# Moving the high and low parts of the weights by 64 bytes in a split-precision transformer kernel

## The chip, the core and the metric

The kernel runs on one core of a Trainium2 chip. The metric is device time in microseconds (us) of one execution, and a kernel's time is the median of its runs. One execution was also recorded by the hardware profiler; all rows below come from it. Engines are named as in the profile: PE (matmul; PEld is its weight load), DVE (vector), ACT (scalar), POOL, SP (here it issues the weight DMAs).

## What is computed

Two transformer blocks in float32, one after the other, on 256 tokens of width 2048; the second adds 16 meta tokens in front.

```python
def first_block(x, c, ...):
    mod = silu(c) @ ada_w + ada_b                     # six vectors: shifts, scales, gates
    h = rms_norm(x) * (1 + sc1) + sh1
    y = hybrid_mixer(h, w_in, ..., w_out)             # attention, gated causal convolution
    x = x + g1 * rms_norm(y)
    h = rms_norm(x) * (1 + sc2) + sh2
    y = (silu(h @ w_gate) * (h @ w_up)) @ w_down      # 2048 -> 5632 -> 2048
    return x + g2 * rms_norm(y)

def second_block(x, meta_tokens, ...):
    r = concatenate([meta, x])                        # 272 rows
    mix = mixer_block(rmsnorm(r), w_in, ..., w_attn_o, pool_w, w_pool_o, w_out)
    r = r + rmsnorm(mix)
    a = causal_dwconv(rmsnorm(r) @ w_up)              # gate and value, 5632 each
    ff = (gelu(gate) * val) @ w_down
    return (r + rmsnorm(ff))[:, 16:]
```

Nearly all the work is the products with the weight matrices.

## The kernel before

Activations lie transposed, features on the 128 partitions and tokens along the free dimension, so a weight tile of 128x128 is the stationary operand of a matmul and 256, 258 or 272 tokens are streamed past it. For float32 accuracy each product is made of three matmuls in the type fp32r: weights and activations are both split into a high part and a low part, and the kernel adds high times high, high weights times low activations, and low weights times high activations.

**The ring.** Weights come in halves of 128x1024 float32 (512 KB): four k-tiles of 256 columns. A half passes three buffers of the same shape, `raw`, `w_hi` and `w_lo`, each a ring of `RING` = 4 slots of 4096 bytes per partition:
- SP loads it into a slot of `raw` (`half`, L340), as soon as the low part that was made from the slot's last content is there.
- ACT copies it, rounded, to `w_hi` (`convert`, L518), once PE is through with the slot.
- DVE subtracts: `w_lo` = `raw` - `w_hi` (L996).
- PE runs 24 matmuls on it: four k-tiles, two column tiles of 128 each, three matmuls each. `half` (from L1591) and `half_one` (from L1730) do so; they differ in where the results go. The three lines are, in order, `w_hi` with high activations, `w_hi` with low activations, `w_lo` with high activations.

There are 836 halves. Before each matmul PE loads its weight tile (128 columns, 512 bytes per partition); the load of the next tile runs while the activations of the matmul before are streamed.

**The order of the work.** Each engine runs its own program, written out by hand, and engines wait for one another by semaphores. Nothing is chosen by a scheduler. The stages and their halves are:

| stage | halves | streamed tiles | columns |
|---|---|---|---|
| first block: gated input, then queries, keys, values | 32 + 48 | `h_hi`, `h_lo` | 256 |
| first block: output projection, attention part | 16 | `a1_hi`, `a1_lo` | 256 |
| first block: output projection, convolution part | 16 | `c_hi`, `c_lo` | 256 |
| first feed-forward: gate and up | 176 | `h_hi`, `h_lo` | 258 |
| first feed-forward: down | 88 | `hid_hi`, `hid_lo` (last chunk `_b`) | 256 |
| second block: queries, keys, values, pool input, forget gate | 66 | `h_hi`, `h_lo` | 272 |
| second block: gates | 64 | `h_hi`, `h_lo` | 258 |
| second block: pool weights and pool projection | 2 + 16 | `pl_hi`, `pl_lo` | 258 |
| second block: attention projection | 16 | `a_hi`, `a_lo` | 258 |
| second block: output projection | 32 | `m_hi`, `m_lo` | 258 |
| second feed-forward: gate and up | 176 | `h_hi`, `h_lo` | 258 |
| second feed-forward: down | 88 | `hid_hi`, `hid_lo` (last chunk `_b`) | 256 |

A feed-forward goes in 11 chunks: gate (8 halves) and up (8 halves) of a chunk, and down (8 halves) of the chunk before.

**Where the buffers lie.** One arena in SBUF holds everything large. It is cut into regions one behind the other: `raw`, `hi`, `lo`, `xt`, `hhi`, `hlo`, `r1`, `r2`, `r3` (L137 to L143), and `place` (L145) puts a tensor at an offset in a region. All sizes before are multiples of 256 bytes, so a tensor's start modulo 256, counted from the arena's start, is that of its offset. Small tensors come behind the arena.
- `raw`, `w_hi` and `w_lo` start at 0 in their regions, and a weight tile starts at a multiple of 512 in them.
- `h_hi`, `h_lo`, `c_hi`, `c_lo`, `a_hi`, `a_lo` have tiles of 272 tokens, 1088 bytes apart: 64 more modulo 256 with each. The 256 real tokens begin 64 bytes into a tile, the 258 live ones 56 bytes.
- `a1_hi`, `a1_lo` have tiles 1024 bytes apart: all at 0.
- `m_hi`, `m_lo`, `pl_hi` and `pl_lo` have tiles 1032 bytes apart: 8 more modulo 256 with each; `pl_lo` begins at 64.
- The tiles of `hid_hi` and `hid_lo` are placed one by one, by the first tuple below in the first feed-forward and by the second in the second; the bases 12288, 16640, 0 and 4352 are multiples of 256.

```python
HID_STEPS = ((192, 1216, 2240, 3264), (160, 1200, 2256, 3296))
```

Of the kernel before, what the change touches and what calls it, by code (L numbers as in the profile page):

```python
# [7 lines left out]
KT = D // 128  # L8
SEQ, META = 256, 16
ALL = SEQ + META  # L10
# [13 lines left out]
RING = 4  # L24
# [104 lines left out]
def build(nc, tokens, params, conv_taps, f_bias, ada_w, w_in, w_out, w_gate, w_up, w_down, w_in_2, w_f_2,  # L129
          w_attn_o_2, pool_w_2, w_pool_o_2, w_out_2, w_ffn_up_2, w_ffn_down_2, out):  # L130
    f32, f32r = mybir.dt.float32, mybir.dt.float32r
    ACT, ALU, AX = mybir.ActivationFunctionType, mybir.AluOpType, mybir.AxisListType
    ctx = ExitStack()
    with ctx:

        base = (nc.sbuf_base + 31) // 32 * 32
        sizes = dict(raw=RING * 4096, hi=RING * 4096, lo=RING * 4096, xt=KT * ALL * 4,  # L137
                     hhi=KT * ALL * 4, hlo=KT * ALL * 4, r1=KT * ALL * 4, r2=38400, r3=40960)
        at, region = 0, {}
        for name, size in sizes.items():  # L140
# [4 lines left out]
        def place(name, reg, off, shape, dt=f32):  # L145
            n = 4
            for s in shape[1:]:
                n *= s
            spans = {"hhi": ("hhi", "hlo")}.get(reg, (reg,))
            assert off + n <= sum(sizes[r] for r in spans), name  # L150
            return nc.alloc_sbuf_tensor_at(name, shape, dt, offset=base + region[reg] + off, align_bytes=4)
# [5 lines left out]
            return ctx.enter_context(nc.semaphore(name))  # L157

        raw = place("raw", "raw", 0, [128, RING, 4, 256])
        w_hi = place("w_hi", "hi", 0, [128, RING, 4, 256], f32r)  # L160
        w_lo = place("w_lo", "lo", 0, [128, RING, 4, 256], f32r)
        xt = place("xt", "xt", 0, [128, KT, ALL])
        h_hi = place("h_hi", "hhi", 0, [128, KT, ALL], f32r)
# [1856 lines left out]
```

## Time and profile before

| | us |
|---|---|
| median of 3 runs | 2722.62 |
| lowest and highest run | 2720.02, 2722.8 |
| profiled execution, its own time | 2717.04 |
| its span, first to last instruction | 2715.2 |
| PE busy in the span | 2609.8 (96%) |
| PE weight loads | 2482.3 (91%) |
| DVE busy | 1707.2 (63%) |
| ACT busy | 1220.3 (45%) |

Busy PE time counts overlapping matmuls once. A matmul's row gives 0.28 us, but the next one starts after some 0.12 us, so how fast PE goes is read from the starts and from how many matmuls stand in a stretch. A window's count has two or three more than started in it, since it takes in those that had begun before.

### The profile page before, as it was taken

How to read it: one execution, taken by the hardware profiler on the slowest of the kernel's cores; microseconds unless marked ns; L12 is line 12 of the kernel's file. 1: busy time of each engine (PE TensorE's matmuls, PEld its weight loads, DVE VectorE, ACT ScalarE, POOL GpSimd, SP SyncE). 2: the span in 40 equal slices, each digit the busy share in tenths (PEclk: the TensorE clock that was granted, in tenths of full speed). 3: DMA queues.
4: the chain of work that ended last, by engine and by line, in shares of the span. 5: the costliest groups of instructions: out<-in, count | busy, mean ns of one | idle time of the engine just before them, and what ended most of it. 6: DMA issues, size and time to landing. Idle time of an engine off the chain costs nothing.

```text
span 2715.2 us, 53794 instructions
## 1 busy us (share of the span) xinstructions
PE 2609.8 (96%) x21278; PEld 2482.3 (91%) x21278; DVE 1707.2 (63%) x2393; ACT 1220.3 (45%) x1649; POOL 49.3 (2%) x98
## 2 busy tenths in 40 slices
PE   5899999899999999998999999999899999999997
PEld 1588887899999999998998899999899999999997
DVE  1388864586666666657655655555676666666667
ACT  1343454544444444445544454444554444444444
POOL 0000000000000000000000000000000000000000
PEclk9799999999999999999999999999999999999999
DMA  9988867576666666565444455555465555555554
GB/s 403 375 309 297 275 204 271 164 244 202 201 203 202 202 202 201 181 185 176 140 145 142 132 155 185 181 182 184 126 193 182 184 184 183 182 183 185 185 173 132
DMA packets 137087, 545.51 MB, mean 201 GB/s; under 512 B 15120, under 2 KB 17424, under 8 KB 124560
## 3 DMA queue, kind: packets, MB, share of 16 engines
q1 hardware_dynamic: 127312, 474.08, 53.5%
q0 software_dynamic: 9216, 67.11, 6.9%
q10 hardware_dynamic: 448, 2.75, 0.3%
q8 instruction: 81, 1.33, 0.2%
q14 instruction: 30, 0.25, 0.0%
HBM read 541.78 MB, written 2.10 MB: 200 GB/s over the span
## 4 chain that ended last, share of the span: by engine, by line
PE 90%; DVE 4%; ACT 3%; DMA 3%; issue 1%; ACTq 0%; DVEq 0%; SPq 0%
PE bank L1608 20%; PE bank L1609 19%; PE bank L1610 19%; PE bank L1745 9%; PE bank L1746 8%; PE bank L1747 8%; PE bank L1644 2%; DMA ada_pre<-in_ada_w 2%; DVE w_lo L996 1%; PE bank L1685 1%; ACT w_hi L518 1%; DVE y L1061 1%; ACT h_hi L594 1%; DMA bf<-in_f_bias 0%; PE bank L1703 0%
## 5 line engine op out<-in xcount | busy, mean ns | idle before, releaser
L996 DVE TENSOR_TENSOR w_lo<-raw,w_hi 128x1024 fp32r<-128x1024 f32 x836 | 1012.5, 1223 | 725.5 <-ACT w_hi L518 724.7
L518 ACT ACTIVATE w_hi<-raw 128x1024 fp32r<-128x1024 f32 x836 | 872.8, 1057 | 914.5 <-PE bank L1610 517.2
L1608 PE MATMUL bank<-h_hi,w_hi 128*128 128x258 f32 (+2 forms) x4112 | 1170.8, 285 | 29.3 <-DVE h_lo L1067 20.4
L1609 PE MATMUL bank<-h_lo,w_hi 128*128 128x258 f32 (+2 forms) x4112 | 1170.2, 285 | 0.0
L1610 PE MATMUL bank<-h_hi,w_lo 128*128 128x258 f32 (+2 forms) x4112 | 1166.1, 284 | 0.0
L1608 PEld LDWEIGHTS bank<-h_hi,w_hi 128*128 128x128 f32 x4112 | 777.7, 189 | 47.4 <-DVE h_lo L1067 22.0
L1610 PEld LDWEIGHTS bank<-h_hi,w_lo 128*128 128x128 f32 x4112 | 779.5, 190 | 0.0
L1609 PEld LDWEIGHTS bank<-h_lo,w_hi 128*128 128x128 f32 x4112 | 779.1, 189 | 0.1
L1746 PE MATMUL bank<-hid_lo,w_hi 128*128 128x256 f32 x1280 | 356.7, 279 | 0.0
L1745 PE MATMUL bank<-hid_hi,w_hi 128*128 128x256 f32 x1280 | 356.5, 279 | 0.0
L1747 PE MATMUL bank<-hid_hi,w_lo 128*128 128x256 f32 x1280 | 356.5, 279 | 0.0
L1746 PEld LDWEIGHTS bank<-hid_lo,w_hi 128*128 128x128 f32 x1280 | 240.9, 188 | 0.0
L1745 PEld LDWEIGHTS bank<-hid_hi,w_hi 128*128 128x128 f32 x1280 | 240.8, 188 | 0.0
L1747 PEld LDWEIGHTS bank<-hid_hi,w_lo 128*128 128x128 f32 x1280 | 240.8, 188 | 0.0
L1306 DVE TENSOR_TENSOR y<-y,bank 128x512 f32<-128x512 f32 x176 | 120.6, 685 | 56.0 <-PE bank L1747 55.5
L1745 PE MATMUL bank<-h_hi,w_hi 128*128 128x256 f32 x384 | 111.0, 289 | 0.0
L1746 PE MATMUL bank<-h_lo,w_hi 128*128 128x256 f32 x384 | 107.1, 279 | 0.0
L1747 PE MATMUL bank<-h_hi,w_lo 128*128 128x256 f32 x384 | 106.9, 278 | 0.0
L1745 PEld LDWEIGHTS bank<-h_hi,w_hi 128*128 128x128 f32 x384 | 72.1, 188 | 16.8 <-issue 15.9
L1644 PE MATMUL bank<-ada_pre,cact 128*32 128x512 f32 x256 | 44.8, 783 | 33.0 <-DMA ada_pre<-in_ada_w 33.0
L758 ACT ACTIVATE hid_hi<-hid 128x256 fp32r<-128x256 f32 x80 | 31.4, 418 | 97.8 <-DVE hid L1329 62.5
L1746 PEld LDWEIGHTS bank<-h_lo,w_hi 128*128 128x128 f32 x384 | 72.2, 188 | 0.1
(225 smaller groups left out, 2637.0 us busy)
## 6 DMA issues: line engine op xcount, KB each, us to landing
raw<-in_w_in SPq DMA_DIRECT2D x208, 512.0 KB, 4.1
raw<-in_w_ffn_up SPq DMA_DIRECT2D x176, 512.0 KB, 4.2
ada_raw<-in_ada_w POOLq DMA_DIRECT2D x64, 1024.0 KB, 6.7
raw<-in_w_gate SPq DMA_DIRECT2D x88, 512.0 KB, 4.0
raw<-in_w_up SPq DMA_DIRECT2D x88, 512.0 KB, 4.2
raw<-in_w_down SPq DMA_DIRECT2D x88, 512.0 KB, 4.2
raw<-in_w_ffn_down SPq DMA_DIRECT2D x88, 512.0 KB, 4.4
ada_pre<-in_ada_w SPq DMA_DIRECT2D x32, 1024.0 KB, 8.6
```

The source lines that it names most:

```text
L518: act.activation(w_hi[:, slot], raw[:, slot], ACT.Copy).then_inc(hi_ready, 1)
L594: act.activation(h_hi[:, kt, cols], xt[:, kt, cols], ACT.Copy, scale=gain[:, kt:kt + 1])\
L758: act.activation(hi[t + o][:, :], hid[:, t + o], ACT.Copy).then_inc(hid_hi_ready, 1)
L996: dve.tensor_tensor(w_lo[:, slot], raw[:, slot], fp(w_hi[:, slot]), ALU.subtract).then_inc(lo_ready, 1)
L1306: dve.tensor_tensor(y[:, 2 * j:2 * j + 2, SB], y[:, 2 * j:2 * j + 2, SB], both(b), ALU.add)\
L1608: pe.matmul(dst, wh, x_hi(kt), start=first and k == 0, stop=False)
L1609: pe.matmul(dst, wh, x_lo(kt), start=False, stop=False)
L1610: mm = pe.matmul(dst, wl, x_hi(kt), start=False, stop=last and k == len(kts) - 1)
L1644: mm = pe.matmul(bank[32 * g:32 * g + 32, b, :], cact[:, kt:kt + 1].to_broadcast([128, 32]), rows[:, slot, 512 * g:512 * g + 512], start=k ...
L1745: pe.matmul(dst, wh, x_hi(kt), start=first and k == 0 and o == 0, stop=False, skip_group_check=True)
L1746: pe.matmul(dst, wh, x_lo(kt), start=False, stop=False, skip_group_check=True)
L1747: mm = pe.matmul(dst, wl, x_hi(kt), start=False, stop=end, skip_group_check=True)
```

## The change

`w_hi` begins 64 bytes into its region. The region `hi` grows by 64 bytes, so `lo` and with it `w_lo` begins 64 bytes further too, and `lo` grows by 192, so that `xt` and all behind it move by 256 bytes. `raw` stays where it is.

```diff
-        sizes = dict(raw=RING * 4096, hi=RING * 4096, lo=RING * 4096, xt=KT * ALL * 4,
+        sizes = dict(raw=RING * 4096, hi=RING * 4096 + 64, lo=RING * 4096 + 192, xt=KT * ALL * 4,
                      hhi=KT * ALL * 4, hlo=KT * ALL * 4, r1=KT * ALL * 4, r2=38400, r3=40960)
...
-        w_hi = place("w_hi", "hi", 0, [128, RING, 4, 256], f32r)
+        w_hi = place("w_hi", "hi", 64, [128, RING, 4, 256], f32r)
         w_lo = place("w_lo", "lo", 0, [128, RING, 4, 256], f32r)
```

The instructions of every engine, their order and their waits are the same in both programs; only addresses differ.

## Rows read from the trace of the kernel before

**Rows 1.** The page: busy time, granted clock by fortieths, and the chain that ended last.

```profile
PE 2609.8 (96%) x21278; PEld 2482.3 (91%) x21278; DVE 1707.2 (63%) x2393; ACT 1220.3 (45%) x1649; POOL 49.3 (2%) x98
...
PEclk9799999999999999999999999999999999999999
...
PE 90%; DVE 4%; ACT 3%; DMA 3%; issue 1%; ACTq 0%; DVEq 0%; SPq 0%
PE bank L1608 20%; PE bank L1609 19%; PE bank L1610 19%; PE bank L1745 9%; PE bank L1746 8%; PE bank L1747 8%; PE bank L1644 2%; DMA ada_pre<-in_ada_w 2%; DVE w_lo L996 1%; PE bank L1685 1%; ACT w_hi L518 1%; DVE y L1061 1%; ACT h_hi L594 1%; DMA bf<-in_f_bias 0%; PE bank L1703 0%
```

**Rows 2.** PE by stretches: length, busy time (matmuls), granted clock, DMA share, GB/s.

```profile
core 0: us, PE busy (x), PEclk, DMA share, GB/s
0.00:100.00 100.00, 58.55 (x304) 0.84 0.96 392
...
396.00:507.00 111.00, 107.50 (x858) 0.98 0.77 262
...
525.00:1280.00 755.00, 750.17 (x6364) 0.99 0.62 199
...
1930.00:2696.00 766.00, 758.62 (x6362) 1.00 0.55 176
2696.00:2715.20 19.20, 3.13 (x18) 0.70 0.32 109
```

**Rows 3.** PE in a down chunk of each feed-forward, a gate/up stretch, the last projection.

```profile
602.95:624.72 21.77, 21.77 (x195) 1.00 0.61 196
2011.12:2033.86 22.74, 22.74 (x194) 1.00 0.63 200
624.72:670.60 45.88, 45.88 (x387) 1.00 0.62 205
1832.19:1923.95 91.76, 91.76 (x770) 1.00 0.59 184
```

**Rows 4.** Timeline of PE, a half of the output projection on `a1`: start, length.

```profile
464.61 0.28 PE L1745 MATMUL bank<-a_hi,w_hi 128*128 128x256 f32 x1
464.73 0.28 PE L1746 MATMUL bank<-a_lo,w_hi 128*128 128x256 f32 x1
...
467.37 0.28 PE L1747 MATMUL bank<-a_hi,w_lo 128*128 128x256 f32 x1
```

**Rows 5.** Timeline of PE, a half of the first input projection on `h`.

```profile
229.08 0.28 PE L1745 MATMUL bank<-h_hi,w_hi 128*128 128x256 f32 x1
...
229.67 0.28 PE L1747 MATMUL bank<-h_hi,w_lo 128*128 128x256 f32 x1
229.78 0.28 PE L1745 MATMUL bank<-h_hi,w_hi 128*128 128x256 f32 x1
...
230.37 0.27 PE L1747 MATMUL bank<-h_hi,w_lo 128*128 128x256 f32 x1
...
230.72 0.28 PE L1747 MATMUL bank<-h_hi,w_lo 128*128 128x256 f32 x1
...
231.06 0.28 PE L1747 MATMUL bank<-h_hi,w_lo 128*128 128x256 f32 x1
...
231.76 0.28 PE L1747 MATMUL bank<-h_hi,w_lo 128*128 128x256 f32 x1
```

**Rows 6.** Weight loads (PEld), by streamed tile: duration in ns, min/median/max.

```profile
L1745 PEld LDWEIGHTS bank<-a_hi,w_hi x128: 186/192/192, 396.7 to 505.7; 128*128 128x128 f32 x128
L1745 PEld LDWEIGHTS bank<-hid_hi,w_hi x1280: 187/188/193, 602.8 to 2673.8; 128*128 128x128 f32 x183
L1745 PEld LDWEIGHTS bank<-h_hi,w_hi x384: 186/188/192, 211.8 to 395.2; 128*128 128x128 f32 x192
```

**Rows 7.** The conversions, by tile (ns, min/median/max) and by line (busy, mean; idle before).

```profile
L518 ACT ACTIVATE w_hi<-raw x836: 1039/1060/1072, 97.7 to 2686.5; 128x1024 fp32r<-128x1024 f32 x168
L996 DVE TENSOR_TENSOR w_lo<-raw,w_hi x836: 1204/1224/1311, 98.8 to 2687.6; 128x1024 fp32r<-128x1024 f32 x168
...
L996 DVE TENSOR_TENSOR w_lo<-raw,w_hi 128x1024 fp32r<-128x1024 f32 x836 | 1012.5, 1223 | 725.5 <-ACT w_hi L518 724.7
L518 ACT ACTIVATE w_hi<-raw 128x1024 fp32r<-128x1024 f32 x836 | 872.8, 1057 | 914.5 <-PE bank L1610 517.2
```

**Rows 8.** What instructions on `w_hi` sat idle for: us, times.

```profile
  PE bank L1747: 382.8, 220
...
  DVE w_lo L996: 11.5, 6
```

## The prediction

> **What bounds the kernel now.** I read the busy shares first. PE is busy 96% of the span, DVE 63%, ACT 45%, and PE's granted clock is at its upper level, 2.4 GHz, in all but the first and the last stretches [rows 1, 2]. The chain that ended last is PE for 90% of the span, and nearly all of that is the six matmul lines of `half` and `half_one` (L1608 to L1610 and L1745 to L1747) [rows 1]. So time is the number of matmuls with ring weights times their pitch, which I take as the distance from one matmul's start to the next one's start. There are 836 halves of 24 matmuls, 20,064 in all: 1 ns more or less on each of them is 20 us, 0.74% of the span. The durations in the rows (276 to 283 ns) are no help here, since matmuls overlap; the starts are.
>
> I then looked at whether the pitch is one number, and it is not. "Distance" below is the start of the streamed tile less the start of the weights, modulo 256. The code gives it without an absolute address, since all region sizes are multiples of 256 bytes.
> - The first feed-forward's down product streams `hid_hi`/`hid_lo` tiles that all lie at distance 192. Its 192 matmuls of a chunk take 21.77 us: 113.4 ns each [rows 3].
> - The second feed-forward's down product runs the same lines with the same 256 columns on tiles at distances 160, 176, 208 and 224: 22.74 us for 192, 118.4 ns [rows 3].
> - The first output projection streams `a1_hi`/`a1_lo`, all at distance 0. From 464.61 to 467.37 there are 23 steps in 2.76 us: 120.0 ns [rows 4].
> - The tiles of `h` are 1088 bytes apart, so they go through four distances, six matmuls on each. In the half that starts at 229.08 they are 64, 128, 192 and 0. Within distance 64 five steps take 0.59 us, within distance 128 five steps take 0.59 us (229.78 to 230.37): 118 ns each. Within distance 192 the last three steps (230.72 to 231.06) take 0.34 us: 113 ns, once more the figure of the down product at 192 [rows 5].
>
> Between the best and the worst of these there are 6.6 ns a matmul at the same clock and the same number of columns, and they go with where the streamed tile starts. L1745 to L1747 write the same PSUM pattern in both the 113.4 and the 120.0 case. DVE and ACT come and go during a chunk, and the pitch does not. What is left is the weights that PE reads at the same time. One row speaks for that directly: the median load of a weight tile takes 192 ns while the `a1` tiles at distance 0 stream, and 188 ns with the `hid` and `h` tiles [rows 6]. The weight tile has the same place in all of them. Only the stream beside it moved, and the load became slower. So I take pitch to be a function of the **distance** between the two, and the change lowers every distance by 64.
>
> **The change part by part**, against the profiled execution (2717.04 us, span 2715.2). Its own time lies 5.6 us under the median of the runs, 2722.62, and I add the sum to the median at the end.
>
> 1. Down product of the first feed-forward: 11 chunks of 8 halves, 2112 matmuls. Distance 192 becomes 128. Pitch now 113.4 [rows 3]; the nearest row for the new distance is the stretch of `h` at 128, 118 ns [rows 5]. It is on the path in full, since one matmul follows the other without idle time in the chunk. 4.6 ns x 2112 = **+9.7 us**.
> 2. Output projection on `a1`: 16 halves, 384 matmuls. Distance 0 becomes 192, so 120.0 becomes 113.4: 6.6 ns x 384 = **-2.5 us**. PE is busy 107.5 of 111 us in that stage [rows 2], so it counts.
> 3. Down product of the second feed-forward: 2112 matmuls, distances 160, 176, 208, 224 become 96, 112, 144, 160. No row has these. The bounds are the best and the worst stretch, 113.4 and 120.0, from 118.4: -10.6 to +3.4 us. I take 118.0, the row at distance 128, which is the middle of the four: **-0.8 us**.
> 4. Everything that streams `h` or `c` tiles (gate and up of both feed-forwards, both input projections, the gates of the second block), and `a` in the second block: the four distances go round in steps of 64, so a shift by 64 gives the same four, in the same cyclic order, beginning one tile later. Their pitch now is 45.88 us for 384, 119.5 ns at 258 columns [rows 3]. **0**, if only the distance counts. This is the largest assumption, since these are over 14,000 of the matmuls: 0.5 ns on them would be 7 us.
> 5. `m` in the last projection (768 matmuls, 91.76 us, 119.5 ns [rows 3]) and `pl` (384, with 48 more for the pool weights): the tiles are 8 bytes apart modulo 256, `m` at distances 0 to 120, which become 192 to 56. Half of these distances are in the row already. The other half (192 to 248) is bounded by 113.4 and 120 again: about 600 matmuls, -3.7 to +0.3 us. I take **0**.
> 6. ACT and DVE: the conversions read `raw` and write `w_hi`, read both and write `w_lo`, each from starts that are now 64 bytes apart. All 836 of each lie within 1039 to 1072 and 1204 to 1311 ns [rows 7], and nothing in the trace shows another distance for them. Within 5% either way they stay hidden: DVE waits 724.7 us for ACT, ACT 900 us for PE to free the slot, and PE waits for `w_lo` 11.5 us in all, in six waits [rows 7, 8]. 60 ns on six exposed waits is 0.4 us. **0**.
> 7. The weight DMAs land in `raw`, which does not move; no instruction is added, removed or reordered; all other buffers move by 256 bytes, and the pitch at 120 does not differ between starts a multiple of 256 apart. **0**.
>
> Sum: 9.7 - 2.5 - 0.8 = **+6.4 us**. Own range, with terms 3 and 5 at their ends: 9.7 - 2.5 - 10.6 - 3.7 = -7 to 9.7 - 2.5 + 3.4 + 0.3 = +11.
>
> The Trainium skill ("SBUF — State Buffer", "SBUF: two separate sides", and the bandwidth table behind it) says that PE has ports of its own that wait for no one, with a second independent read port for weight loads. By that rule moving the weights would do nothing, and the sum would be 0. The 192 against 188 ns of the load [rows 6] speaks against it here, though no run of before has the weights elsewhere. It is the first rival.
>
> **The rivals.**
> - **Only the streamed tile's own place counts** (or something else that this change leaves). Then weights may lie anywhere, every pitch stays, and the time is 2722.6. For it: every row has the weights at one place, so the trace cannot separate distance from place. Against it: the same stream length, lines and PSUM pattern give 113 and 120 ns, and the load of an unmoved weight tile changes with the stream. Chance 0.16.
> - **The second down product falls on a good distance.** The same mechanism, with term 3 (and the new half of term 5) near 113.4: -10.6 and -3.7 beside +9.7 and -2.5 gives -7 us, 2715.5. A step of 6.6 ns between distances 64 bytes apart is seen, so a place between 96 and 160 can be that good. Against: the two measured neighbours on this side, 64 and 128, are both at 118. The point from which it decides is 117.9 ns less 3 ns: under about 115.4 ns there the sum is negative. Chance 0.15.
> - **More than the distance counts: the start of the weights itself.** Slower, by much. The weights then begin 64 bytes off what they were in a memory whose pieces may be larger than 64 bytes, and each 512-byte tile touches one piece more. A price for touching more comes from the width: 258 columns on `h` take 119.5 ns [rows 3] and 256 columns 116.5 (23 steps from 229.08 to 231.76 [rows 5]); two columns in 256 are 0.9 ns of that, so 2 ns are left over for the longer and oddly placed run. Half of that, for a load that is the shorter of the two reads, on 20,064 matmuls is +20 us: 2743. It decides from 0.3 ns per matmul on. For it: term 4 stands on symmetry and on no row. Against: streams that begin at 64 and at 192 are no slower than those at 0 and 128. Chance 0.14.
> - The change does what it says: sizes and offsets shift exactly the two tensors by 64 and all behind them by 256. A rival is not needed there.
>
> **How the numbers follow.** The forecast has 0.55: 2722.6 + 6.4 = 2729. A change under 0.2% (5.4 us) cannot be told from none. Of the forecast's 0.55, 0.32 lies over +5.4 us, 0.2 within, 0.03 under -5.4. The first rival is within (0.16), the second is faster (0.13) or within (0.02), the third slower (0.14). Together: faster 0.16, same 0.38, slower 0.46. The range runs from the second rival's 2715 to a little over the third's centre, 2744, which leaves out about 0.1 above, and 0.05 to 0.1 below.
>
> **What the profile of the changed kernel would show.** Step 1: a chunk of the first down product takes 22.6 us in place of 21.77. Step 2: the `a1` steps are 113 ns, and their weight loads 188 ns. Step 3: the second down product's chunk, anywhere from 21.8 to 23.0 us. Step 4: 384 matmuls of gate and up still take 45.9 us. This is the row to look at first, since it holds most of the matmuls: if it moved, distance alone was not the whole story. Step 6: medians of 1060 and 1224 ns. If the chunk of step 1 stays at 21.77 and `a1` at 120, the weights' place does not matter. The prediction is wrong outside 2715 to 2744.

## The result, and the profile after

| | before | changed |
|---|---|---|
| median (12 runs each) | 2718.45 us | 2730.76 us |
| lowest and highest | 2713.99, 2726.89 | 2724.79, 2732.22 |
| ratio | | 1.0038 (95%: 1.0028 to 1.0047) |
| span of the profiled execution | 2715.2 us | 2723.6 us |

The changed kernel is slower by 0.38%, some 10 us. (The medians lie 12.3 us apart, the means of the runs 10.1.) The predicted time was 2729, from +6.4 us on a median of 2722.6; the median of before over these 12 runs is 2718.45.

The busy shares and the chain are those of before. The first two lines are the chain, the last two the conversions (busy, mean ns, idle before).

```profile
PE 90%; DVE 4%; ACT 3%; DMA 3%; issue 1%; ACTq 0%; DVEq 0%; SPq 0%
PE bank L1608 20%; PE bank L1609 19%; PE bank L1610 19%; PE bank L1745 9%; PE bank L1747 9%; PE bank L1746 9%; PE bank L1644 2%; DMA ada_pre<-in_ada_w 2%; DVE w_lo L996 1%; PE bank L1685 1%; ACT w_hi L518 1%; DVE y L1061 1%; DMA bf<-in_f_bias 1%; ACT h_hi L594 1%; PE bank L1703 0%
...
L996 DVE TENSOR_TENSOR w_lo<-raw,w_hi 128x1024 fp32r<-128x1024 f32 x836 | 1012.5, 1223 | 724.2 <-ACT w_hi L518 723.4
L518 ACT ACTIVATE w_hi<-raw 128x1024 fp32r<-128x1024 f32 x836 | 873.4, 1057 | 922.4 <-PE bank L1610 512.7
```

ACT and DVE do the same work in the same time as in [rows 7]. What moved is the distance between matmul starts. Three stretches of PE after: a down chunk of the first and of the second feed-forward, and 384 matmuls of gate and up. They answer to the first three lines of [rows 3].

```profile
600.34:623.12 22.78, 22.78 (x194) 1.00 0.61 187
2020.01:2042.69 22.68, 22.68 (x195) 1.00 0.63 201
623.12:669.01 45.89, 45.89 (x387) 1.00 0.64 205
```

The first down chunk went from 21.77 to 22.78 us (118.6 ns). Over all 11 chunks the steps add up to +11.4 us, since the ninth lost more than the others (see below). The second went from 22.74 to 22.68: -0.7 us. Gate and up kept their 45.9 us. The `a1` half (timeline: start, length), which answers to [rows 4]:

```profile
464.34 0.28 PE L1745 MATMUL bank<-a_hi,w_hi 128*128 128x256 f32 x1
...
466.94 0.28 PE L1747 MATMUL bank<-a_hi,w_lo 128*128 128x256 f32 x1
```

23 steps in 2.60 us are 113 ns, where [rows 4] has 2.76 us and 120. That would be -2.6 us for 16 halves. Halves that begin after a stop take a few steps to reach the 113 ns, and over all steps of the stage the sum is -2.2 us. The weight loads of `a1` fell from a median of 192 ns in [rows 6] to 188, the figure of the others:

```profile
L1745 PEld LDWEIGHTS bank<-a_hi,w_hi x128: 186/188/190, 397.3 to 504.3; 128*128 128x128 f32 x128
```

I added up the steps within each half over the whole trace, with halves that contain a stop put in at the mean of the others. All stages together give +8.5 us. With the steps between halves taken in as well (all steps under 200 ns) it is +9.7; the stops between are 2.3 us shorter and the first of these matmuls begins 0.9 us later, which makes the 8.4 us by which the span grew.

### The profile page after: what moved, and what is told of

The parts are those of the page before. It is cut to its first block, busy times and chain, and to the rows that moved or that the text cites. A ratio compares the mean times of both kernels' runs of the same rounds, so it can differ in the third digit from the quotient of the medians.

```text
span 2723.6 us, 53794 instructions
## 1 busy us (share of the span) xinstructions
PE 2616.1 (96%) x21278; PEld 2489.6 (91%) x21278; DVE 1707.2 (63%) x2393; ACT 1220.9 (45%) x1649; POOL 49.3 (2%) x98
## 4 chain that ended last, share of the span: by engine, by line
PE 90%; DVE 4%; ACT 3%; DMA 3%; issue 1%; ACTq 0%; DVEq 0%; SPq 0%
PE bank L1608 20%; PE bank L1609 19%; PE bank L1610 19%; PE bank L1745 9%; PE bank L1747 9%; PE bank L1746 9%; PE bank L1644 2%; DMA ada_pre<-in_ada_w 2%; DVE w_lo L996 1%; PE bank L1685 1%; ACT w_hi L518 1%; DVE y L1061 1%; DMA bf<-in_f_bias 1%; ACT h_hi L594 1%; PE bank L1703 0%
## 5 line engine op out<-in xcount | busy, mean ns | idle before, releaser
L1746 PE MATMUL bank<-hid_lo,w_hi 128*128 128x256 f32 x1280 | 360.0, 281 | 0.0
L1747 PE MATMUL bank<-hid_hi,w_lo 128*128 128x256 f32 x1280 | 359.8, 281 | 0.0
L1745 PE MATMUL bank<-hid_hi,w_hi 128*128 128x256 f32 x1280 | 359.5, 281 | 0.0
L1745 PEld LDWEIGHTS bank<-hid_hi,w_hi 128*128 128x128 f32 x1280 | 241.2, 188 | 0.0
L1746 PEld LDWEIGHTS bank<-hid_lo,w_hi 128*128 128x128 f32 x1280 | 240.8, 188 | 0.0
L1747 PEld LDWEIGHTS bank<-hid_hi,w_lo 128*128 128x128 f32 x1280 | 240.8, 188 | 0.0
L1745 PE MATMUL bank<-h_hi,w_hi 128*128 128x256 f32 x384 | 110.8, 289 | 0.0
L1747 PE MATMUL bank<-h_hi,w_lo 128*128 128x256 f32 x384 | 107.4, 280 | 0.0
L1746 PE MATMUL bank<-h_lo,w_hi 128*128 128x256 f32 x384 | 107.3, 280 | 0.0
L1745 PEld LDWEIGHTS bank<-h_hi,w_hi 128*128 128x128 f32 x384 | 72.2, 188 | 16.8 <-issue 15.9
L1746 PEld LDWEIGHTS bank<-h_lo,w_hi 128*128 128x128 f32 x384 | 72.4, 188 | 0.1
```

The costliest lines, as they stand in the source:

```text
L1745: pe.matmul(dst, wh, x_hi(kt), start=first and k == 0 and o == 0, stop=False, skip_group_check=True)
L1746: pe.matmul(dst, wh, x_lo(kt), start=False, stop=False, skip_group_check=True)
L1747: mm = pe.matmul(dst, wl, x_hi(kt), start=False, stop=end, skip_group_check=True)
```

## The experiments

In all of them "distance" is the start of the streamed tile less that of the weights, modulo 256, as in the prediction. A ratio is that to the kernel before, with its 95% interval. Where there was one run, it stands beside the median of before taken with it, and I rely on the trace alone. The window rows have the columns of [rows 3].

### Does the distance count, or the place? (arena_64)

```diff
-        base = (nc.sbuf_base + 31) // 32 * 32
+        base = (nc.sbuf_base + 31) // 32 * 32 + 64
...
-        ctx.enter_context(nc.sbuf_tensor("arena", [128, at + 32], mybir.dt.uint8))
+        ctx.enter_context(nc.sbuf_tensor("arena", [128, at + 96], mybir.dt.uint8))
```

> Every buffer of the kernel before, raw and the weights and the streamed tiles and the small ones, begins 64 bytes further, so all distances are those of before while all places modulo 256 are new. Distance theory: the kernel before again, first down chunk 21.77 us, second 22.74, a1 steps 120.0 ns, time within 0.1% (2718 us). Rival, the weights' own place modulo 256 counts (or modulo 128): the first down chunk goes to the 22.8 us of the changed kernel and the time to about 2729 us.

2717.41 us, ratio 0.9993 (0.9982 to 1.0005). The two down chunks:

```profile
601.37:623.14 21.77, 21.77 (x194) 1.00 0.65 196
2009.55:2032.29 22.74, 22.74 (x194) 1.00 0.66 201
```

They are those of before to the hundredth, and the steps of all stages together differ by less than 0.1 us. Here the weights have the places of the changed kernel modulo 256, and nothing is slower. So this place of the weights costs nothing by itself; what the change did, it did through the places of weights and streams against one another.

### Which of two weights does a stream meet? (hi_only_64)

The diff is that from the kernel before.

```diff
-        sizes = dict(raw=RING * 4096, hi=RING * 4096, lo=RING * 4096, xt=KT * ALL * 4,
+        sizes = dict(raw=RING * 4096, hi=RING * 4096 + 256, lo=RING * 4096, xt=KT * ALL * 4,
...
-        w_hi = place("w_hi", "hi", 0, [128, RING, 4, 256], f32r)
+        w_hi = place("w_hi", "hi", 64, [128, RING, 4, 256], f32r)
```

> w_hi alone begins 64 bytes further; w_lo keeps its place modulo 256, and so does all else. In the down product of the first feed-forward (streams at distance 192 from unmoved weights: 113.4 ns per matmul before, 118.8 with both parts moved) the two kinds of weights now lie at distances 128 (w_hi) and 192 (w_lo). Theory A, a stream collides with the weight load that runs beside it, which is that of the next matmul: the steps that follow L1745 and L1747 (next load from w_hi) are near 119, the step that follows L1746 (next load from w_lo) near 113; a chunk takes about 22.4 us. Theory B, a stream is slowed by where its own weights lie: the steps after L1745 and L1746 (own weights w_hi) are near 119, the one after L1747 near 113; the chunk takes the same 22.4 us, but the slow steps are others. Theory C, only the difference between w_hi and w_lo or the average over a triple counts: all three steps alike. Whole kernel: about +6 us against before for A and B.

2729.53 us in one run, before 2719.04. The first down chunk takes 22.78 us and gate and up 45.98:

```profile
601.27:624.05 22.78, 22.78 (x194) 1.00 0.64 189
624.05:670.03 45.98, 45.98 (x386) 1.00 0.64 204
```

Both theories A and B missed. Neither has its slow and fast steps: the means over the first chunk by line are 119.0 (after L1745), 119.2 (L1746) and 117.8 ns (L1747), with no step under 115. That the three are nearly alike is what theory C said, and no more than that. It is no average of the two distances either, since 128 for `w_hi` and 192 for `w_lo` give 22.78 us, as much as 128 for both. The stages on `h` lost 1.6 ns at 256 columns and 0.4 at 258, the four distances now being mixed in pairs. The one run is 10.5 us over before, where about 6 was expected. A step's length may then depend on the steps before it, and the next experiments take that up.

### Restoring the distance does not restore the pitch (w64_hid64, w64_hid_both)

Both start from the changed kernel. The diff is that of w64_hid_both; w64_hid64 has the first tuple alone.

```diff
-HID_STEPS = ((192, 1216, 2240, 3264), (160, 1200, 2256, 3296))
+HID_STEPS = ((256, 1280, 2304, 3328), (256, 1280, 2304, 3328))
```

> The changed kernel, with the hid tiles of the first feed-forward 64 bytes further too, so that their distance to the weights is 192 again. Distance theory: the first down chunk is back at 21.77 us (11.4 us less in all), a1 stays at 113.3 ns (2.5 us less than before), the second down product as in the changed kernel (0.4 us less than before): about 2.9 us under before, 2716 us. If the weights' own place costs something in the down product, the chunk stays near 22.8 us and the time near 2729 us.

> As w64_hid64, and the hid tiles of the second feed-forward lie at distance 192 as well. Distance theory: its down chunk goes from 22.70 to 21.77 us, 0.93 us in each of 11 chunks, 10 us less: about 13 us under before, 2705 us (-0.5%). If the second feed-forward's down product has a bound of its own (DVE does more there), its chunk stays over 22 us.

w64_hid64: 2730.67 us, ratio 1.0044 (1.0028 to 1.0061). w64_hid_both: 2725.82 us, 1.0025 (1.0016 to 1.0035). The first and second down chunk, of w64_hid64 and then of w64_hid_both:

```profile
600.56:623.18 22.62, 22.62 (x195) 1.00 0.64 191
2022.66:2045.34 22.68, 22.68 (x195) 1.00 0.64 198
```

```profile
599.96:622.58 22.62, 22.62 (x195) 1.00 0.62 190
2022.10:2044.72 22.62, 22.62 (x195) 1.00 0.67 204
```

This is the miss that taught most. At distance 192 the down product takes 22.62 us, 117.8 ns, in three places where I expected 21.77, while the `a1` stretch of the same kernels, also at distance 192, has its 113.3 ns. So a distance has more than one steady pitch. How a chunk begins shows it. Timeline of PE, the kernel before, then w64_hid64; the first row is the first matmul on a hid tile, after a stretch of 258 columns on `h`:

```profile
602.95 0.28 PE L1745 MATMUL bank<-hid_hi,w_hi 128*128 128x256 f32 x1
...
603.41 0.28 PE L1746 MATMUL bank<-hid_lo,w_hi 128*128 128x256 f32 x1
...
603.87 0.28 PE L1747 MATMUL bank<-hid_hi,w_lo 128*128 128x256 f32 x1
```

```profile
600.56 0.28 PE L1745 MATMUL bank<-hid_hi,w_hi 128*128 128x256 f32 x1
...
601.03 0.28 PE L1746 MATMUL bank<-hid_lo,w_hi 128*128 128x256 f32 x1
...
601.50 0.28 PE L1747 MATMUL bank<-hid_hi,w_lo 128*128 128x256 f32 x1
```

Steps 5 to 8 take 0.46 us in the one and 0.47 in the other. In nanoseconds the trace has 118, 116, 114, 113, 114, 113 in the first and 122, 115, 117, 118, 118, 117 in the second, and each keeps its pitch for the 192 matmuls. The code and the distance modulo 256 are the same. One thing that differs is the stretch before: it ends at distance 248 in the kernel before and at 184 with the weights moved. That is theory E: how the streams stand to each other when a stretch begins decides which of two cycles it falls into.

One chunk speaks for an effect of the entry with nothing moved. The ninth down chunk of the first feed-forward is entered not from `h` but from eight small matmuls of 4 columns. The first rows show them, in the timeline of the changed kernel, and the last seven halves (168 matmuls) of the chunk behind them. The next three have these halves in w64_hid64, in the kernel before and in hid_160_224, a run described below.

```profile
1150.86 0.95 PE L1658 MATMUL bank<-ident,rows_sb 128*128 128x4 f32 x8
...
1154.63:1174.79 20.16, 20.16 (x171) 1.00 0.59 183
```

```profile
1153.41:1173.20 19.79, 19.79 (x171) 1.00 0.62 185
```

```profile
1148.96:1168.00 19.04, 19.04 (x170) 1.00 0.63 192
```

```profile
1153.82:1173.76 19.94, 19.94 (x171) 1.00 0.58 184
```

In the changed kernel the same tiles at distance 128 run at 120.0 ns in this chunk and at 118.6 in the eight before it; at distance 160 it is 118.7 and 117.3. So one set of places has more than one pitch at these distances too. But the same chunk speaks against the two ends named above, 248 and 184, as the whole reason: here the small matmuls stand between, and w64_hid64 still runs at 117.8 and the kernel before at 113.3.

A rival is left. The changed kernel and all that start from it also move everything behind the weights by 256 bytes. Modulo 512 the high hid tiles are at distance 192 and the low ones at 448 in the kernel before, and the other way round in w64_hid64. No run tells this from the entry.

w64_hid64's ratio stands for 12 us (8 to 17), and its steps for 6.5. Some of the rest is seen in its trace: the granted clock was 0.98 in the projections of the second block, where it was 1.00 before, and the stage took 3.1 us longer. The first row is w64_hid64's, the second the one of before for the same halves.

```profile
1328.32:1540.54 212.22, 210.16 (x1556) 0.98 0.47 144
```

```profile
1321.44:1530.59 209.15, 207.07 (x1556) 1.00 0.47 146
```

Why the clock fell there I did not find out. w64_hid_both has the same dips.

### Entry against place (w64_first128, w64_parity)

Another rival to theory E is theory P: in the hid tiles, high and low part lie an odd multiple of 256 bytes apart, and in the `a1`, `h` and `c` tiles an even one. The first kernel gives each half another entry, the second takes that difference away. Both start from the changed kernel.

```diff
-HID_STEPS = ((192, 1216, 2240, 3264), (160, 1200, 2256, 3296))
+HID_STEPS = ((192, 1280, 2304, 3328), (160, 1200, 2256, 3296))
```

```diff
-HID_STEPS = ((192, 1216, 2240, 3264), (160, 1200, 2256, 3296))
+HID_STEPS = ((256, 1280, 2304, 3328), (160, 1200, 2256, 3296))
...
-        hid_parts = [[hid_tiles(f"hid_{name}_{part}", reg, first, HID_STEPS[part])
+        hid_parts = [[hid_tiles(f"hid_{name}_{part}", reg, first - 256 * (name == "hi" and part == 0), HID_STEPS[part])
```

> As w64_hid64 (first down product at distance 192, 117.8 ns where 113.4 was expected), but the first of the four hid tiles lies at distance 128, the other three at 192. Theory E, distance 192 has two steady pitches, 113.3 and 117.8, and which of them a stretch falls into depends on what it comes from: entered from distance 128 it goes 122, 116, 114, 113 as in the input projection before, so the twelve last matmuls of each half run at 113 and a half's mean is near 115.3 ns (chunk 22.1 us). Theory P, in this place 192 is simply worth 117.8 (the high and low tiles lie 256 bytes apart modulo 512, or some other place counts): the mean stays at 117.8 or above (chunk 22.6 us or more).

> As w64_hid64, but the high hid tiles of the first feed-forward's main chunks begin 256 bytes earlier, so that high and low tiles have the same place modulo 512, as the a1, h and c tiles have. Theory P (modulo 512 counts between high and low tile): first down chunk at 21.77 us, 113.4 ns. Theory E (entry decides): nothing of that counts, 117.8 ns again, 22.62 us.

One run each: 2719.27 and 2721.68 us, before 2719.74. The first down chunk of w64_first128, and a half of it; then the chunk of w64_parity:

```profile
601.96:624.09 22.13, 22.13 (x194) 1.00 0.60 192
```

```profile
604.73 0.28 PE L1745 MATMUL bank<-hid_hi,w_hi 128*128 128x256 f32 x1
...
605.44 0.28 PE L1745 MATMUL bank<-hid_hi,w_hi 128*128 128x256 f32 x1
...
606.13 0.28 PE L1745 MATMUL bank<-hid_hi,w_hi 128*128 128x256 f32 x1
...
607.49 0.28 PE L1745 MATMUL bank<-hid_hi,w_hi 128*128 128x256 f32 x1
```

```profile
600.24:622.86 22.62, 22.62 (x195) 1.00 0.64 192
```

P falls, and what E says of the entry is borne out: three of the four tiles have not moved against w64_hid64. Entered from distance 128, they are in the fast cycle, 12 steps from 606.13 to 607.49 in 1.36 us, 113.3 ns; entered as there, they take 117.8. Here a tile at the poor distance 128 (six steps in 0.71 us) makes the down product shorter by 5.4 us than four tiles at the good one (22.13 against 22.62 us, eleven times). Taking the odd 256 bytes between high and low away did nothing, 22.62 us again. It brought the high tiles alone back to distance 192 modulo 512, so that rival stays open for the low ones; the places do not settle the pitch, but they may have a say in which cycle an entry leads to.

### One distance for all k-tiles (rows_128, rows_120)

From the kernel before; rows_120 has OFF = 120 and the hid tiles 8 bytes earlier. The diff shows the main lines: the region sizes, the subtraction on DVE and the matmuls of PE are fitted to the new layout too.

```diff
+ROW = RING * 256 + 16
+OFF = 128
...
-HID_STEPS = ((192, 1216, 2240, 3264), (160, 1200, 2256, 3296))
+HID_STEPS = ((64, 1152, 2240, 3328), (64, 1152, 2240, 3328))
...
-        w_hi = place("w_hi", "hi", 0, [128, RING, 4, 256], f32r)
-        w_lo = place("w_lo", "lo", 0, [128, RING, 4, 256], f32r)
+        w_hi = place("w_hi", "hi", OFF, [128, 4, ROW], f32r)
+        w_lo = place("w_lo", "lo", OFF, [128, 4, ROW], f32r)
...
-                act.activation(w_hi[:, slot], raw[:, slot], ACT.Copy).then_inc(hi_ready, 1)
+                act.activation(w_hi[:, :, 256 * slot:256 * slot + 256], raw[:, slot], ACT.Copy).then_inc(hi_ready, 1)
```

> The weights are laid out by k-tile, with 64 bytes between the rows (k-tile k of every slot begins at 128 + 64k modulo 256), so that the four k-tiles of a half keep one distance to the h tiles, which also go on by 64: 192 in the 256-column stages, 184 in the 258-column stages, 128 in the 272-column one; the hid tiles are placed to be at 192. Distance theory: the 256-column stages on h go from 116.8 to 113.4 (-3.4 ns on 96 halves, -8 us), the second down product to 113.4 or 117.8 (-11 or -1 us), the first at 113.4 or 117.8 (0 or +9 us), and the 258-column stages, half of the kernel, settle on one pitch in place of the mixture of 119.4; from the steps of before within that stretch (115 to 124 ns) it may be anywhere in that span: -40 to +40 us. Rival, the pitch depends on the weights' own place too: no stage becomes uniform.

> As rows_128, with the weights 8 bytes earlier and the hid tiles with them: distance 192 for the 258-column stages on h, 200 for the 256-column ones, 136 for the 272-column ones, 192 for hid. Distance theory: hid as in rows_128 if only distances count; the 258-column stages at 192: 113.4 + 0.9 = 114.3 ns if a run of 258 settles as one of 256 does, which would be 5 ns less on 416 halves, 50 us; if the longer run moves the phase from one matmul to the next, they keep a mixture near 119.

rows_128: 2725.05 us, 1.0018 (1.0008 to 1.0028). rows_120: 2736.81 us, 1.0058 (1.0036 to 1.0080). A down chunk and 384 matmuls of gate and up, of rows_128 and of rows_120:

```profile
601.40:623.86 22.46, 22.46 (x194) 1.00 0.61 190
623.86:669.73 45.87, 45.87 (x386) 1.00 0.65 205
```

```profile
603.04:626.23 23.19, 23.19 (x195) 1.00 0.59 185
626.23:672.00 45.77, 45.77 (x386) 1.00 0.63 204
```

Gate and up did settle in rows_120 (distance 192), on a pattern of six steps that repeats with each k-tile (117, 116, 119, 123, 121, 119 ns in this stretch, 115, 121, 121, 120, 120, 118 in the half before the down chunk), but its mean is 119.2. In rows_128 (184) the pattern repeats only with each half, at 119.4. These runs of 258 columns did not lock on 113 at distance 192. By their steps the 258-column stages on `h` changed by 0.1 us in rows_128, where I had left 40 either way, and by -2.2 in rows_120, where I had held 50 us less possible. The 256-column stages on `h`, at distance 192 in rows_128, were a miss as well: 116.9 ns for the 113.4 expected. The hid tiles at distance 192 from their own weights did not run at 113 either: 117.0 ns in rows_128, and 120.8 in rows_120 (120.3 in every second chunk), though all distances of this stage are those of rows_128. What differs is the stretch it is entered from, and that weights and hid tiles begin 8 bytes earlier; no run separates the two. In this layout the load beside the last stream of a k-tile is that of the next k-tile, 64 bytes further on, so the distance to it is 128 once in six steps. That the load of the next tile is the partner fits this, but I have not shown it apart from the own weights; it stays open.

### How wide is 192? (hid_184_200, hid_176_208, hid_160_224)

From the kernel before, all four hid tiles at one distance, another in each feed-forward. The diff is that of hid_184_200.

```diff
-HID_STEPS = ((192, 1216, 2240, 3264), (160, 1200, 2256, 3296))
+HID_STEPS = ((184, 1208, 2232, 3256), (200, 1224, 2248, 3272))
```

> The same at distances 184 and 200, 8 bytes to either side of 192. If a stretch's pitch is set by pieces of 16 bytes or more, one of the two (the side on which no border is crossed) is at 113.4 exactly; if it moves with every column, both lie between 113.4 and the pitches at 176 and 208.

> The kernel before, with all four hid tiles at distance 176 in the first feed-forward and at 208 in the second. If collisions come in pieces of 64 bytes, both pitches are near those of 192 or of the next 64 (113 to 118); if in pieces of 16, neighbours of 192 differ little from it: 112 to 115 ns. Two-pitch theory: a stretch at one distance settles within six matmuls on a short cycle whose mean is constant over the chunk. Whole kernel: -1 to -11 us for the second down product at 118.4 to 113.4, 0 to +9 us for the first.

> The same at distances 160 and 224. The curve between the 118 of distance 128, 113.4 at 192 and 120 at 0 has its low somewhere between; if the low is broad, 160 or 224 is under 116 ns; if 192 is a narrow notch, both are at 117 to 120. Any distance under 113.4 would be the one to use for both feed-forwards.

2733.29, 2728.38 and 2722.82 us in one run each, before 2717.36. The down chunks of first and second feed-forward, in the order of the expectations:

```profile
601.88:624.92 23.04, 23.04 (x194) 1.00 0.65 187
2024.00:2047.04 23.04, 23.04 (x195) 1.00 0.61 197
```

```profile
601.66:624.55 22.89, 22.89 (x194) 1.00 0.62 190
2020.86:2043.73 22.87, 22.87 (x195) 1.00 0.61 198
```

```profile
601.62:624.14 22.52, 22.52 (x194) 1.00 0.64 190
2016.97:2039.69 22.72, 22.72 (x194) 1.00 0.65 203
```

| distance | 160 | 176 | 184 | 192 | 200 | 208 | 224 |
|---|---|---|---|---|---|---|---|
| ns per matmul | 117.3 | 119.2 | 120.0 | 113.4 | 120.0 | 119.1 | 118.3 |

The figure for 192 is that of the kernel before. A smooth curve and pieces of 16 bytes, as the first two expectations had it, are out; the third had named a narrow notch, with 117 to 120 at 160 and 224, and that is what came. From this entry 192 is a notch, and 8 bytes to either side of it every step behind the first seven of a chunk is 120 ns, as at distance 0. None of these distances beat 113.4. But each was measured from the `h` stretch at distance 248. The other entry of the ninth chunk left 176 and 184 as they are and made 118.7 of the 117.3 at 160. As 192 itself has 117.8 in other kernels, the others may have faster cycles that no run here entered.

### The fast cycle wherever it can be had (all_192)

```diff
-HID_STEPS = ((192, 1216, 2240, 3264), (160, 1200, 2256, 3296))
+HID_STEPS = ((192, 1216, 2240, 3264), (192, 1216, 2240, 3264))
...
-        a1_hi = place("a1_hi", "r2", 0, [128, AT, SEQ], f32r)
-        a1_lo = place("a1_lo", "r2", 8192, [128, AT, SEQ], f32r)
+        a1_hi = place("a1_hi", "r2", -64, [128, AT, SEQ], f32r)
+        a1_lo = place("a1_lo", "r2", 8128, [128, AT, SEQ], f32r)
```

> The kernel before (weights unmoved) with the hid tiles of the second feed-forward at distance 192 too, as those of the first are, and the a1 tiles 64 bytes earlier, at 192 in place of 0. Entry theory: the second down product is entered from the same stretch as the first (gate and up at 248 with 258 columns), so it falls into the fast pitch: 113.4 for 118.4 ns on 2112 matmuls, 10.7 us less; the a1 stretch goes from 119.9 to 113.3 as in the changed kernel, 2.5 us less. Together 13.2 us under before, ratio 0.9951, about 2705 us. If the second feed-forward enters otherwise and falls into 117.8, only 1.3 + 2.5 us are won, ratio 0.9986.

2709.05 us, ratio 0.9958 (0.9945 to 0.9972). The down chunks:

```profile
598.31:620.08 21.77, 21.77 (x195) 1.00 0.64 195
2006.53:2028.29 21.76, 21.76 (x194) 1.00 0.65 209
```

It is faster than both kernels. The second down product is entered from the same stretch as the first, and falls into the same cycle: 0.98 us less in each of 11 chunks. With the `a1` stage the steps sum to -12.9 us, where -13.2 was expected. The time of 2709 missed the 2705 named, but -13.2 us lies within the interval of the ratio (-15 to -8 us). Here nothing behind the weights moved, so the gain on `a1`, 119.9 to 113.5 ns, comes from the 64 bytes alone.

## Why the prediction was right, point by point

- **The number** was hit partly by luck. The sum was added to 2722.6, a median of three runs, and the median over 12 runs is 4 us lower; the change was put at +6.4 and measured at about 10 (7.6 to 12.8). The two errors nearly cancel in 2729 against 2731.
- **The basis**, that pitch goes with the distance between streamed tile and weights: confirmed as far as it goes. arena_64 moved both and nothing changed; the changed kernel moved the weights by 64 bytes against the streams, the hid kernels the streams alone, and the pitch changed in both. The first rival (the place of the stream alone) is out, and so is the third (the weights' own place). The Trainium skill ("SBUF — State Buffer", "SBUF: two separate sides", and the bandwidth table behind it) says that PE's SBUF port never waits on anyone, and gives PE a second independent read port for weight loads. By that rule the prediction had a sum of 0 as a rival, and that is not what came: the first down product went from 113.4 to 118.6 ns. The load time that the prediction took as its direct sign is a poor one, though. At distance 184 the pitch is 120.0 ns with a median load of 188:

```profile
L1747 PEld LDWEIGHTS bank<-hid_hi,w_lo x62: 187/188/191, 602.0 to 624.0; 128*128 128x128 f32 x62
```

- **Step 1**, the first down product: +9.7 forecast, +11.4 measured. The term was mis-sized. I took 118 ns from five steps within `h` at 128, and a long stretch there runs at 118.6, in a cycle of 115 to 122 ns that five steps are too few to show; in the ninth chunk it runs at 120.0. This makes up about half of what the sum was short of (9.7 us by all steps, 6.4 forecast).
- **Step 2**, `a1`: -2.5 forecast, -2.2 measured over all its steps, with the pitch (113 ns) and the loads (188 ns) as named.
- **Step 3**, the second down product: -0.8 forecast, -0.7 measured. That it fits is luck: 118.0 was the row of one distance, used for four others, and hid_184_200 shows that 8 bytes can make 6.6 ns. The bounds (-10.6 to +3.4) were the honest part.
- **Step 4**, the stages with four distances, over 14,000 matmuls: 0 forecast, some +1 us measured, and 45.89 us for 45.88 in gate and up. In the half that starts at 229.25 the steps of before come back one k-tile later. The second k-tile starts at 229.96, the fourth at 231.36:

```profile
229.25 0.28 PE L1745 MATMUL bank<-h_hi,w_hi 128*128 128x256 f32 x1
...
229.96 0.28 PE L1745 MATMUL bank<-h_hi,w_hi 128*128 128x256 f32 x1
...
230.54 0.28 PE L1747 MATMUL bank<-h_hi,w_lo 128*128 128x256 f32 x1
...
231.36 0.28 PE L1745 MATMUL bank<-h_hi,w_hi 128*128 128x256 f32 x1
...
231.60 0.28 PE L1747 MATMUL bank<-h_hi,w_lo 128*128 128x256 f32 x1
...
231.94 0.28 PE L1747 MATMUL bank<-h_hi,w_lo 128*128 128x256 f32 x1
```

  Distance 64 has moved from the first k-tile to the second (five steps in 0.58 us), and 192 from the third to the fourth (the last three in 0.34, as in [rows 5]). Within a half the order of the distances is another, and the mean without the step between halves is 117.1 for 116.8 at 256 columns, +0.7 us, given back by -0.9 at 258 and 272. With the steps between halves it is +1.1 and -0.2: that part was put at nothing, and is 1 us.
- **Steps 5 to 7**: `m` and `pl` +0.2 to +0.3 us by their steps; conversions unchanged; nothing that stands out from the DMAs. The granted clock was also below its upper level from 507 to 525 us (0.74), beside the first and last stretches that the prediction names; no term rests on that.
- **The second rival** (the second down product on a good distance) did not come about, but its point was real: all_192 has it, for 10.7 us, by places that this change does not give.
- What was **wrong** in the reasoning, without harm to the forecast: that a distance has one pitch. For the change itself this cost little, since its 192 stretch on `a1` fell into the fast cycle. Had the change restored the hid distance too, I would have forecast 2716, and it took 2731 (w64_hid64).

The steps give +8.5 us within the halves and +9.7 with those between. The ratio gives 10 (7.6 to 12.8), so they agree within the interval. Why the pitch follows the distance at all no run shows; what PE's two reads do to each other is not in the trace.

## What to carry to other kernels

When PE is the bound and matmuls follow one another without a gap, read their starts, not their lengths: the same instruction went at 113 to 120 ns here, 6% of the rate, by where its two operands lay to each other and by what had run before it. Moving a ring of weights moves its distance to every tile that streams against it, so look for tiles that all have one distance, since those change as a block, while tiles that step through all distances average out. Try places on the chip rather than work them out, for what a stretch comes from counts as well, and 8 bytes can make the difference.

## What the runs showed of the hardware that was not expected

- Back-to-back matmuls of 256 columns, with a 128x128 fp32r weight load beside each and the granted clock at 1.00, had steady pitches from 113.3 to 120.0 ns with all tiles at one distance. The median weight load took 188 ns at 113.3 and at 117.8; at 120.0 it took 192 at distance 0, 191 at 200 and 188 at 184.
- At distance 192 both 113.3 and 117.8 were seen, the first also with tiles that ran at 117.8 in another kernel (w64_first128). Which one came was set within six matmuls of the entry and kept over 192. At distance 128 the changed kernel had 118.6 and 120.0 on the same tiles.
- From a stretch at distance 248 the fast pitch sat in a notch: 113.4 ns at 192, 120.0 at 184 and at 200.
- Moving everything by 64 bytes changed nothing, so it is the places against one another that count. That they count modulo 256 and not modulo 512 is not shown: the one run that moved a stream by 256 (w64_parity, the high tiles) changed nothing, from the slow cycle.
- Runs of 258 columns did not lock at constant distance 184 or 192: they kept a pattern that repeats with each half or each k-tile, with a mean of 119.4 and 119.2 ns.
